# Expert weights of a mixture-of-experts step: one of three loads per expert moved from SyncE's DMA queue to ScalarE's

## The reference, cut to what matters

```python
def expert_block(args):
    xblk, e = args
    gu = xblk @ w_gate_up[e] + b_gate_up[e]
    gate, up = gu[:, :D_FF], gu[:, D_FF:]
    gate = jnp.minimum(gate, SWIGLU_LIMIT)
    up = jnp.clip(up, -SWIGLU_LIMIT, SWIGLU_LIMIT)
    glu = gate * jax.nn.sigmoid(SWIGLU_ALPHA * gate)
    return ((up + 1.0) * glu) @ w_down[e] + b_down[e]
```

## Time and profile before

| | us |
|---|---|
| median of 3 runs | 1208.43 (1208.03 to 1210.14) |
| the profiled execution, its own time | 1208.28 |
| span from the first to the last instruction in it | 1206.5 |
| TensorE busy | 1184.6 |
| VectorE, ScalarE busy | 433.4, 265.5 |

### The profile page before, as it was taken

One profiled execution on the slowest core, in us unless ns is written; L12 is line 12 of the kernel. 1 busy time (PEld: TensorE's weight loads), 2 busy tenths in 40 slices (PEclk: granted clock), 3 DMA queues, 4 the chain that ended last, 5 costly groups with the idle time before them and its releaser, 6 DMA issues.

```text
span 1206.5 us, 17611 instructions
## 1 busy us (share of the span) xinstructions
PE 1184.6 (98%) x7502; PEld 570.7 (47%) x7502; DVE 433.4 (36%) x947; ACT 265.5 (22%) x641; POOL 41.6 (3%) x100
## 2 busy tenths in 40 slices
PE   8999999999999999999999999999999999999996
PEld 6777777645344344434444444344444434343332
DVE  3357846553423332332323234122332332222324
ACT  3114547332121111211121211111111111121213
POOL 8000100100000000000000000000000000000000
PEclk9999999999999999999999999999999999999999
DMA  9932202599999999999999999999999999999996
GB/s 287 253 106 71 81 3 78 194 403 348 404 431 426 428 412 428 425 433 431 432 428 430 434 431 432 427 431 429 433 430 430 431 431 430 432 423 426 426 423 227
DMA packets 50393, 436.06 MB, mean 361 GB/s; under 512 B 11637, under 2 KB 27064, under 8 KB 31882
## 3 DMA queue, kind: packets, MB, share of 16 engines
q1 hardware_dynamic: 49188, 431.74, 87.0%
q0 software_dynamic: 960, 3.02, 0.8%
q10 hardware_dynamic: 166, 0.15, 0.0%
HBM read 430.01 MB, written 4.89 MB: 360 GB/s over the span
## 4 chain that ended last, share of the span: by engine, by line
PE 90%; DMA 8%; DVE 1%; issue 0%; SPq 0%; ACT 0%; DVEq 0%
PE bank L1647 34%; PE bank L1683 17%; PE bank L922 10%; PE bank L1613 8%; DMA ring<-in_w_gate_up 5%; PE bank L1717 4%; PE bank L1408 3%; PE bank L1674 3%; DMA ring<-in_w_down 3%; PE bank L1708 1%; PE bank L909 1%; PE bank L955 1%; DMA ring<-in_w_in 1%; PE bank L1188 0%; PE bank L1172 0%
## 5 line engine op out<-in xcount | busy, mean ns | idle before, releaser
L1647 PE MATMUL bank<-ring,mix 128*64 128x512 f32 x1504 | 344.8, 598 | 3.1 <-DMA ring<-in_w_gate_up 2.8
L1647 PEld LDWEIGHTS bank<-ring,mix 128*64 128x64 f32 x1504 | 101.3, 136 | 200.7 <-issue 196.1
L1683 PE MATMUL bank<-ring,mix 128*64 128x512 f32 x736 | 168.2, 598 | 1.2 <-DMA ring<-in_w_down 1.2
L2998 DVE TENSOR_TENSOR hTb<-bank,w2a 128x512 f32<-128x512 f32 x32 | 22.1, 692 | 360.8 <-PE bank L1674 360.8
L2245 ACT ACTIVATE mix<-bank,nf 128x256 f32<-128x256 f32 x64 | 26.9, 470 | 431.2 <-PE bank L1613 431.1
L922 PE MATMUL bank<-hTb,ring 128*128 128x328 f32 (+1 forms) x416 | 119.7, 442 | 0.2 <-issue 0.2
L1647 PE MATMUL bank<-mix 128*64 128x512 f32 x500 | 112.7, 595 | 2.8 <-issue 2.7
L3058 DVE TENSOR_TENSOR mix<-mix,bank 128x512 f32<-128x512 f32 x70 | 48.2, 688 | 160.8 <-PE bank L1717 144.8
L922 PEld LDWEIGHTS bank<-hTb,ring 128*128 128x128 f32 x416 | 77.5, 191 | 33.8 <-issue 2.2
L1683 PEld LDWEIGHTS bank<-ring,mix 128*64 128x64 f32 x736 | 49.3, 136 | 90.4 <-issue 83.3
L1647 PEld LDWEIGHTS bank<-mix 128*64 128x64 f32 x500 | 35.3, 137 | 72.6 <-issue 71.5
(11 more groups left out here) (450 smaller groups left out, 1075.2 us busy)
## 6 DMA issues: line engine op xcount, KB each, us to landing
ring<-in_w_gate_up SPq DMA_DIRECT2D x27, 4096.0 KB, 22.5
ring<-in_w_gate_up SPq DMA_DIRECT2D x38, 2048.0 KB, 18.0
ring<-in_w_down SPq DMA_DIRECT2D x13, 4096.0 KB, 23.7
ring<-in_w_down SPq DMA_DIRECT2D x18, 2048.0 KB, 16.9
mix<-in_w_gate_up SPq DMA_DIRECT2D x9, 4096.0 KB, 22.7
mix<-in_w_gate_up SPq DMA_DIRECT2D x13, 2048.0 KB, 14.7
mix<-in_w_down SPq DMA_DIRECT2D x5, 4096.0 KB, 25.4
ring<-in_w_in SPq DMA_DIRECT2D x14, 1024.0 KB, 5.8
```

What stands on the lines that cost most here:

```text
L1647: last_ = mm(b_[64 * half:64 * half + 64, :].rearrange("s (p q) -> s p q", q=4), toks, cols[:, half], start=(c == 0), stop=(c == KT - 1))
L1683: last_ = mm(b_[r:r + 64, :], lhs, w[:, o:o + NCOL], start=(j == 0 and q == 0), stop=(j == 1 and q == 3))
```

## The change

For the experts 10 to 27 the first gate and up pair, U(e)a, is no longer issued by SyncE. ScalarE issues it in `down_out(e - 3)`, behind its wait for the down products of expert e - 3, whose place the pair takes, and ahead of its wait for the gate column and of y_high. `BY_SCALAR` maps the expert whose down products are awaited to the piece that is loaded: 18 entries, 7 to piece 58 (U10a), up to 24 to piece 160 (U27a). Place, source, size and semaphore of each transfer stay as they were, and SyncE's other loads keep their waits and their order.

```diff
+BY_SCALAR = {PIECES[HELD[k + 1]][1]: k for k in WIDE if k % 2 == 0 and PIECES[HELD[k + 1]][0] == "down"}
...
                 if k in WIDE:
-                    if k % 2 == 0:
+                    if k % 2 == 0 and k not in BY_SCALAR.values():
                         sync.wait_ge(S("w_used"), HELD[k + 1] + 1)
                         load(wpair[SLOT[k] // 2], rows_in(kind, e, j, 2), f"w{SLOT[k]}_in")
                     return
...
             def down_out(e):
 
                 act.wait_ge(S("w_used"), PLACE["down", e, NDN - 1] + 1)
+                if e in BY_SCALAR:
+                    k = BY_SCALAR[e]
+                    kind, x, j = PIECES[k]
+                    rows = wdn[:, x, :] if kind == "down" else wgu4[:, x, j // 2, :]
+                    act.dma_start(wpair[SLOT[k] // 2], rows).then_inc(S(f"w{SLOT[k]}_in"), 16)
                 act.wait_ge(S("gates_out"), e // 2 + 1)
```

More of the change, by code:

```diff
@@ L559, in build @@
         wpair = [at(2048 * n, 2 * PIECE) for n in (8, 0, 4)] + [mix[:, 13 * W5 - 2 * PIECE:13 * W5]]
+        wgu4 = A["w_gate_up"][0].rearrange("e (j p r) n -> p e j (r n)", j=2, r=4)
+        wdn = A["w_down"][0].rearrange("e (p q) n -> p e (q n)", q=8)
         yrow = [ring[:, 0:DM], ring[:, DM:2 * DM], ring[:, 2 * DM:2 * DM + 512]]
@@ L650, in _ @@
             wgu2 = A["w_gate_up"][0].rearrange("e (j p r) n -> p e j (r n)", j=4, r=2)
-            wgu4 = A["w_gate_up"][0].rearrange("e (j p r) n -> p e j (r n)", j=2, r=4)
-            wdn = A["w_down"][0].rearrange("e (p q) n -> p e (q n)", q=8)
             def rows_in(kind, e, j, n=1):
```

## The result

Over 13 runs each, the kernel before has a median of 1208.84 us and the changed one 1212.14 us. The medians differ by 3.3 us. The ratio is 1.0032 (95% interval 1.0025 to 1.0040), which is some 3.9 us slower. 1214.3 was forecast. The profiled execution of after took 1212.99 us with a span of 1211.3, 4.8 longer than the span before.

A forecast was written before the change was run, and what follows sets the result against it. Saturated DMA transfers were taken to bound the expert phase. 9.0 us lost at expert 25's down pair less 3.0 given back made +6.0 on 1208.28, so 1214.3 us; own range 1211 to 1216, overall 1208 to 1216.5.

The forecast's parts named there:

- What bounds: Expert phase: saturated transfers set the pace, 9.7 us a pair at 430 GB/s; only their order can change.
- The issue at nothing: ScalarE's issue ahead of y_high: 0.55 us each under 2.11 us of cover before the scatter, cost 0.
- Equal shares: Moved load shares the engines equally with SyncE's queue, lands within 19.5 us, delays loads ahead by up to 9.7 us.
- Rival A: Landing order costs nothing, expert 25's down pair hardly late: 1208.3 us, up to 1210.7; chance 0.15.
- B: Two queues move more than one, each pair landing sooner; 0.17 us off each gives near 1206; chance 0.08.
- C: ScalarE's load gets less than an equal share and becomes the late one: near 1220 us; chance 0.06.
- rival D: Moved load gets over half the engines; expert 25's down pair still 9.7 us late: near 1215; a forecast variant, no separate chance.
- The loss that counts, 9.0 us: Expert 25's down pair lands at 1044.1, not 1034.4, so TensorE starts it 9.0 us late.
- 1044.1 - x: Landing of expert 25's down pair if ScalarE's last moved load is issued x us behind 1024.7; x at most 2.3.
- both cases end alike: Whether TensorE is on time or 6 us late, expert 25's down pair is wholly shared and lands at 1044.1.
- The earlier losses: Waits for down pairs of experts 13, 15, 21, 23, first 2.3 us; TensorE some 6 us late by expert 25's; not summed.
- What is given back, 3.0 us: Waits of before vanish at expert 27's gate and up pairs (0.79, 0.65) and in the tail (1.5): 3.0 us.

The follow-up runs named there:

- The swap on one queue: No load on ScalarE; SyncE issues expert 25's down pair behind expert 27's first gate and up pair; against the kernel before: 1218.36 us, ratio 1.0077.
- The one run made for this cost: All big loads on SyncE, ScalarE issues a 2 KB transfer at the same 18 places; against the kernel before: 1210.13 us, ratio 1.0014.
- fourteen moved loads: Only 14 of the 18 loads moved, those of experts 10 to 23; against the kernel before: 1208.75 us, ratio 1.0002.
- the run with one load: Only one of the 18 loads moved, expert 27's first gate and up pair; against the kernel before: 1217.18 us, ratio 1.0068.
- The repeat of after: The changed kernel profiled a second time, nothing altered: 1212.44 us.

## Why the prediction was right

**What bounds.** Right: the engines stay at 1.00 and 431 GB/s, and what changed is the order of landing. The swap on one queue gives the same loss without a second queue.

**The issue at nothing.** Right in after, as far as the traces show. The issue takes 0.33 us on ScalarE (not the 0.55 of the only row before), y_high starts 0.44 later, the scatter does not move. The rows of after that answer to the earlier trace rows:

```profile
698.44 0.33 ACTq L2320 DMA_DIRECT2D ring<-in_w_gate_up  x1
698.88 1.38 ACT L2326 ACTIVATE y_high<-bank,gc 64x512 fp32r<-64x512 f32 x2 [2.72 <-PE bank L1684]
700.29 1.52 DVE L3032 SCALAR_TENSOR_TENSOR y_low<-bank,gc,y_high 64x512 fp32r<-64x512 f32 x2 [2.11 <-ACT y_high L2326]
...
703.48 0.73 PE L1718 MATMUL bank<-y_high,slot_rows 128*128 128x512 f32 x2
```

The cover of 2.11 us is 1.67 now. The one run made for this cost was 1.7 us slower from a cause not shown; fourteen moved loads at +0.1 us (at most 1.3 by the interval) are the better evidence.

**Equal shares.** Right as a rule of turns, and only roughly right as a number. In the run with one load the shares are 47.6% for ScalarE's queue and 53.0% for SyncE's. In after, from the start of sharing to the landing of D25, ScalarE's queue has clearly more than half (window 1026.7 to 1041.8):

```profile
q10 hardware_dynamic: 117, 3.83, 59.0%
q1 hardware_dynamic: 99, 2.72, 41.9%
```

The repeat of after has 56.3 to 44.7 in nearly the same window. Why it is not half stays open. Rival A (no effect) falls, as D25 lands 7.4 us late; B (more bandwidth), as 100.1% stays 100.1%; C, as ScalarE's load gets more than half and not less. The share in after is that of rival D. But D's time was near 1215, with D25 still 9.7 late, and it was named a variant of the forecast; the mechanism is the same. The moved loads take 23.8 us to landing and not 19.5.

**The loss that counts, 9.0 us.** The mechanism held, the size did not: 6.8. The mis-sized step is "it shares the sixteen engines with them from its issue on". The queue of after in the 3.3 us behind ScalarE's issue of U27a at 1023.36:

```profile
q1 hardware_dynamic: 46, 1.38, 97.9%
```

ScalarE's queue has no packet there. TensorE was 5.6 us late by then (1023.36 to 1017.76, as I had assumed with 6), so the sharing began at 1026.8, and U26b had landed at 1024.5. D25 thus had a stretch of the engines to itself. With equal shares that is 2.3 us, the other 7.4 take 14.8, and D25 lands at 1041.6; 1041.85 was measured. (The prediction's own formula, 1044.1 - x, gives 1042.0 if x is counted from the first packet and not from the issue.) This agreement is partly luck, since two things in it cancel. SyncE's queue did not have half of the engines but 41.9%: of D25's 4.19 MB at most 2.72 started behind 1026.7. So at least 1.47 MB, 3.4 us' worth and not 2.3, had started before. The trace does not tell which packets of SyncE's queue are D25's; that its first ones run on some engines while the last of U26b still run on others would give this, but it is argued.

In the run with one load TensorE was in time, sharing began ahead of D25, and it landed at 1044.1 as worked out. So my sentence that both cases end alike was wrong, and the missing term is the time from the issue to the first packet.

**The earlier losses.** Expected were 1.5 to 3 us at D13, D15, D21, D23, D25. In after TensorE waits for down pairs at D14, D15, D20 to D25, 0.4 to 1.5 us each; D13 had none. Smaller and more of them. That they come to 5.6 us at U27a's issue, where I had assumed 6, is luck: the places and sizes were others, and TensorE was 1.0 us later than in before at 524 already, ahead of the first moved load. The sum used no term of these, but the place of D25 does hang on when U27a is issued.

**What is given back, 3.0 us.** 1.6 and 1.8, so 3.4. Sum by measured terms: 6.8 - 3.4 = +3.4, and +1.4 for the clock behind the branch in this one execution, 4.8 in the span. The forecast of +6.0 was thus too high by 2.2 for D25 and by 0.4 for what comes back. The medians' +3.3 and the ratio's +3.9 lie near the 3.4, but a pair of profiles cannot confirm it closer than to a microsecond or so: the two spans of the kernel before differ by 1.4.

## What to carry to other kernels

When the DMA engines are saturated, a second queue brings no bandwidth but changes the order: a load on it takes about half of the engines' time from what is in line. Look for the load with the least slack among those overtaken, and for the last one of them, since later waits erase what came before. Here the loads until expert 23 could be moved for nothing that could be measured, and the last one alone cost 8 us; so undo a change of this kind from its end, not by thinning it out.

## What the hardware did that I had not expected

- With SyncE's queue full, the first packet of ScalarE's load starts late: 3.4 us behind the issue of U27a, and 3.4 to 3.9 for 16 of the 18 moved loads of after (1.7 and 2.3 for the other two). The one late store of ScalarE in before, at 1203.35, with no load of weights in line, only other stores, had its first packet after 1.9 us. Whether it is the full queue that makes the rest was not tested. The Trainium skill ("DMA: Bandwidth & Descriptors", Specifications) gives about 0.6 us to the first byte for the path that SyncE and ScalarE use; the measured numbers decide here.
- A wait of TensorE for data can cost more than itself. Behind waits of 3.06, 4.37 and 9.03 us the granted clock stood at half (1.2 GHz), and 16 products took 5.01 and 6.09 us for 3.65, 32 took 8.78 for 7.04; behind one of 3.70 it did not fall. Of all twelve waits for data from 2.0 to 9.0 us between 530 and 1195 in the 14 profiles, that one alone had no such stretch. Behind the branch, 2.4 to 3.3 us without work, it fell in 7 of 14 profiles, at 1.4 to 1.7 us each.
- The kernel with 18 small transfers in place of the moved loads, 2592 packets of 16 bytes among saturated ones, was slower by 0.14% (0.05% to 0.23%). Which part of it costs this was not shown.
